# Stick-breaking attention: one log/softplus buffer per head parity, gate chunks split a step sooner, and TensorE's filler work in another order

## What is computed

```
z = einsum('bhqd,bhkd->bhqk', q, k) * scale
log_1m = where(strict, log_sigmoid(-z), 0)
tail = cumsum(log_1m, axis=3, reverse=True) - log_1m
a = where(strict, exp(log_sigmoid(z) + tail), 0)
sb = einsum('bhqk,bhkd->bhqd', a, v)
merged = sig(g_sb)*(sb @ w_up_sb) + sig(g_pl)*(pl @ w_up_pool) + sig(g_xa)*(xa @ w_up_x)
x += merged @ w_out ;  x += HierMoE(RMSNorm(x)) ;  out = RMSNorm(x)
```

## Time and profile before

| | before |
|---|---|
| median of 3 runs | 760.4 us (759.59 to 760.98) |
| profiled execution, its own time | 760.23 us |
| its span, first to last instruction | 758.5 us |
| mean granted TensorE clock | 0.972 |
| PE busy | 699.3 us (92%), 3547 matmuls |
| DVE busy | 514.1 us (68%) |
| ACT busy | 413.8 us (55%) |

### The profile page before, as it was taken

How to read it: one execution, slowest core, us unless ns; L and a number is a source line. 1 busy time by engine, 2 the same in 40 slices (tenths; PEclk the granted TensorE clock), 3 DMA queues, 4 the chain that set the end, 5 groups by cost and what they waited for, 6 DMA issues and landing times.

```text
span 758.5 us, 9936 instructions
## 1 busy us (share of the span) xinstructions
PE 699.3 (92%) x3547; PEld 583.3 (77%) x3547; DVE 514.1 (68%) x563; ACT 413.8 (55%) x428; POOL 109.6 (14%) x112
## 2 busy tenths in 40 slices
PE   4999999979799999999999989999999999999920
PEld 3898888878688888888888948888888888888810
DVE  5878755665534326071544588999999999999927
ACT  6726675675442323131233337777777778777712
POOL 5000000000000000000000130333433443331120
PEclk9999999998899999999999999999999999999975
DMA  8552330000042232233476369999999999999444
GB/s 282 170 167 56 111 111 1 1 28 2 15 149 87 83 111 79 87 97 125 165 264 236 122 217 393 394 388 370 367 375 369 366 376 366 385 366 375 181 170 189
DMA packets 85169, 155.47 MB, mean 205 GB/s; under 512 B 6229, under 2 KB 37071, under 8 KB 84628
## 3 DMA queue, kind: packets, MB, share of 16 engines
q1 hardware_dynamic: 78452, 137.39, 51.2%
q0 software_dynamic: 6688, 17.69, 6.2%
HBM read 150.64 MB, written 12.58 MB: 215 GB/s over the span
## 4 chain that ended last, share of the span: by engine, by line
PE 83%; DVE 6%; ACT 5%; issue 3%; DMA 2%; POOL 1%; POOLq 0%; DVEq 0%; ACTq 0%
PE ps L481 24%; PE ps L482 24%; PE ps L483 24%; PE ps L1536 2%; PE ps L1276 1%; PE ps L1278 1%; DVE soft L1826 1%; PE ps L1593 1%; PE ps L1462 1%; PE ps L1562 1%; PE ps L1490 1%; DMA y_rows<-ye,y_col 1%; ACT log_in L911 1%; ACT log_in L909 1%; ACT soft_hi L917 1%
## 5 line engine op out<-in xcount | busy, mean ns | idle before, releaser
L454 DVE TENSOR_TENSOR ring_lo<-raw_a,ring_hi 128x2048 fp32r<-128x2048 f32 (+2 forms) x58 | 115.5, 1995 | 103.6 <-ACT ring_hi L448 103.6
L454 DVE TENSOR_TENSOR ring_lo<-raw,ring_hi 128x2048 fp32r<-128x2048 f32 x71 | 161.4, 2289 | 12.3 <-ACT ring_hi L448 11.0
L448 ACT ACTIVATE ring_hi<-raw 128x2048 fp32r<-128x2048 f32 x71 | 136.2, 1920 | 19.8 <-PE ps L483 19.8
L481 PE MATMUL ps<-hT_hi,ring_hi 128*128 128x512 f32 x288 | 114.3, 397 | 5.3 <-ACT attn L923 3.4
L448 ACT ACTIVATE ring_hi<-raw_a 128x2048 fp32r<-128x2048 f32 (+2 forms) x58 | 97.4, 1680 | 32.3 <-PE ps L483 32.3
L483 PE MATMUL ps<-hT_hi,ring_lo 128*128 128x512 f32 x288 | 113.1, 393 | 0.0
L482 PE MATMUL ps<-hT_lo,ring_hi 128*128 128x512 f32 x288 | 113.1, 393 | 0.0
L481 PE MATMUL ps<-ring_hi,xT_hi 128*128 128x512 f32 x240 | 94.8, 395 | 1.8 <-DVE xT_lo L2039 1.8
L483 PE MATMUL ps<-ring_hi,xT_lo 128*128 128x512 f32 x240 | 93.8, 391 | 0.0
L482 PE MATMUL ps<-ring_lo,xT_hi 128*128 128x512 f32 x240 | 93.7, 390 | 0.0
L481 PEld LDWEIGHTS ps<-hT_hi,ring_hi 128*128 128x128 f32 x288 | 54.6, 190 | 17.8 <-ACT attn L923 3.6
(11 more groups left out here) (347 smaller groups left out, 1230.4 us busy)
## 6 DMA issues: line engine op xcount, KB each, us to landing
raw<-in_w_down SPq DMA_DIRECT2D x25, 1024.0 KB
raw<-in_w_gate SPq DMA_DIRECT2D x47, 512.0 KB
raw<-in_w_up SPq DMA_DIRECT2D x47, 512.0 KB
raw_a<-in_w_in SPq DMA_DIRECT2D x15, 1024.0 KB
raw_a<-in_w_gate SPq DMA_DIRECT2D x17, 512.0 KB
raw_a<-in_w_up SPq DMA_DIRECT2D x17, 512.0 KB
raw_a<-in_w_down SPq DMA_DIRECT2D x7, 1024.0 KB
raw_a<-in_w_in SPq DMA_DIRECT2D x10, 512.0 KB, 7.5
```

What stands on the lines that cost most here:

```text
L448: act.activation(ring_hi[:, c[0] % SPLIT, 0:width], buf[:, 0:width], ACT.Copy).then_inc(hi_ready, 1)
L454: dve.tensor_tensor(ring_lo[:, s, 0:width], buf[:, 0:width], ring_hi[:, s, 0:width].bitcast(F32), ALU.subtract).then_inc(lo_ready, 1)
L481: pe.matmul(out_ap, l_hi, r_hi, start=start, stop=False, skip_group_check=True)
```

## The change

Five things are edited. (1) `log_in` goes; the three passes of `logarithm(n)` and the softplus work in `soft[n % 2]`, with `soft_lo[n % 2]` on it, so that the two heads of a pair have a buffer each. `softplus` no longer waits for `tails(n-1)`; `soften` does instead, for `soft_hi`, which still exists once. (2) On DVE the softplus of an odd head is issued at the end of the pair before, not at the start of its own, and on ACT `soften(b)` stands ahead of `weigh(a)`. (3) The splits of chunks 10 and 11 move from the end of pairs 1 and 2 to their middle, ahead of `weigh(b)`, and `value_hi` and `value_lo` behind the logarithm and the softplus. (4) `fill_b` is cut in two at k = 2: 6 of its 24 matmuls (`CUT`) stand ahead of `values(b)`, 18 behind it; in pair 0 `project_v(2)` and `project_qk(5)` change places. (5) The gate half of the last pair goes to bank 7, the values of heads 6 and 7 to banks 2 and 3 (`value_bank`); the gate half waits for `value_sum(5)`, 15 of its 24 matmuls stand ahead of `tails(7)` and 9 behind `values(6)`. The number of matmuls is the same; ACT and DVE have one instruction less in each round of the gated sum, a pair of 512 columns becoming one of 1024.

```diff
@@ -210,9 +210,8 @@
     pool_a = sb("pool_a", [P, 2, U0 + S], F32, "t", 16 * KB + 8448)
     probs = [sb("probs0", [P, 8, MEM], F32, "m", 32 * KB), sb("probs1", [P, 8, MEM], F32, "t", 16 * KB)]
 
-    log_in = sb("log_in", [P, ZW], F32, "t", 0)
-    soft = sb("soft", [P, ZW], F32, "t", 5 * KB)
-    soft_lo = sb("soft_lo", [P, ZW], F32R, "t", 5 * KB)
+    soft = [sb(f"soft{b}", [P, ZW], F32, "t", 5 * b * KB) for b in range(2)]
+    soft_lo = [sb(f"soft_lo{b}", [P, ZW], F32R, "t", 5 * b * KB) for b in range(2)]
     soft_hi = sb("soft_hi", [P, ZW], F32R, "t", 10 * KB)
     attn_hi = sb("attn_hi", [P, ZW], F32R, "t", 15 * KB)
     attn = [sb(f"attn{b}", [P, ZW], F32, "t", (20 + 5 * b) * KB) for b in range(2)]
@@ -268,7 +267,10 @@
     def bank(b, n=1):
         return ps[:, 512 * b:512 * (b + n)]
 
-    GATE_BANK = ((6, 2), (0, 1), (4, 5))
+    GATE_BANK = ((6, 7), (0, 1), (4, 5))
+
+    def value_bank(m):
+        return bank(7 if m < HEADS - 2 else m - 4)
 
     def gate_pair(g):
 
@@ -904,17 +906,18 @@
             def logarithm(n):
 
                 act.wait_ge(z_ps, n + 1)
-                if n > 0:
-                    act.wait_ge(z_soft, n)
-                act.activation(log_in[:, :], scores(n), ACT.Abs).then_inc(act_c, 1)
+                buf = soft[n % 2]
+                act.activation(buf[:, :], scores(n), ACT.Abs).then_inc(act_c, 1)
                 act.wait_ge(act_c, 2 * n + 1)
-                act.activation(log_in[:, :], log_in[:, :], ACT.Exp, scale=-1.0).then_inc(act_c, 1)
+                act.activation(buf[:, :], buf[:, :], ACT.Exp, scale=-1.0).then_inc(act_c, 1)
                 act.wait_ge(act_c, 2 * n + 2)
-                act.activation(log_in[:, :], log_in[:, :], ACT.Ln, bias=1.0).then_inc(z_ln, 1)
+                act.activation(buf[:, :], buf[:, :], ACT.Ln, bias=1.0).then_inc(z_ln, 1)
 
             def soften(n):
                 act.wait_ge(z_soft, n + 1)
-                act.activation(soft_hi[:, :], soft[:, :], ACT.Copy).then_inc(soft_h, 1)
+                if n > 0:
+                    act.wait_ge(tail_ps, n)
+                act.activation(soft_hi[:, :], soft[n % 2][:, :], ACT.Copy).then_inc(soft_h, 1)
 
             def weigh(n):
                 act.wait_ge(tail_ps, n + 1)
@@ -937,14 +940,16 @@
             qk_hi(4, 6)
             for p in range(HEADS // 2):
                 a, b = 2 * p, 2 * p + 1
+                soften(b)
                 weigh(a)
-                soften(b)
                 if p == 0:
-                    qk_hi(5, 6)
+                    v_hi_part(2, 6)
                 if p == 1:
                     qk_hi(6, 6)
+                    split_hi(act, K(C_MERGE))
                 if p == 2:
                     v_hi_part(3, 6)
+                    split_hi(act, K(C_MERGE + 1))
                 weigh(b)
                 value_x(a)
                 if p < HEADS // 2 - 1:
@@ -952,18 +957,14 @@
                 value_x(b)
                 if p < HEADS // 2 - 1:
                     soften(a + 2)
-                value_hi(a)
-                value_hi(b)
                 if p == 0:
-                    v_hi_part(2, 6)
+                    qk_hi(5, 6)
                 if p == 1:
                     qk_hi(7, 6)
                 if p < HEADS // 2 - 1:
                     logarithm(b + 2)
-                if p == 1:
-                    split_hi(act, K(C_MERGE))
-                if p == 2:
-                    split_hi(act, K(C_MERGE + 1))
+                value_hi(a)
+                value_hi(b)
 
 
             act.preload_act_table_set("sigmoid_and_others")
@@ -1202,10 +1199,12 @@
                                         start=False, stop=m == MB - 1, skip_group_check=True)
                 ins.then_inc(xo_ps, 1)
 
-            def project_qk(n, b):
+            def project_qk(n, b, k0=0, k1=KD):
 
                 wh, wl = chunk(K(C_PAIR[n // 2]))
-                proj(b, wh, wl, 1024 * (n % 2), P).then_inc(chunk_used if n % 2 else q_ps, 1)
...
@@ -1283,7 +1282,7 @@
 
                 pr = m // 2
                 pe.wait_ge(a_l, m + 1)
-                if m >= 1:
+                if 1 <= m < HEADS - 2:
                     pe.wait_ge(av_sum, m)
                 if m == 0:
                     pe.wait_ge(v_l, 2)
...
@@ -1335,39 +1334,32 @@
 
             pe.wait_ge(xo_sum, 2)
             project_qk(4, 6)
-            def gate_part(k0, k1):
-
-                wh, wl = chunk(K(C_MERGE))
-                for k in range(k0, k1):
-                    o = P + k * 256
-                    ins = three(pe, bank(GATE_BANK[0][1]), wh[:, o:o + P], wl[:, o:o + P], hT_hi[:, k, :], hT_lo[:, k, :],
-                                k == 0, k == KD - 1)
-                return ins
+            CUT = 2
 
             def fill_a(p):
                 if p == 0:
                     pe.wait_ge(qk_l, 5)
-                    project_qk(5, 6)
+                    project_v(2, 6)
                 if p == 1:
-                    pe.wait_ge(v_l, 3)
+                    pe.wait_ge(qk_l, 6)
                     project_qk(6, 6)
                 if p == 2:
                     pe.wait_ge(qk_l, 8)
                     project_v(3, 6)
                 if p == 3:
-                    pe.wait_ge(a_exp, HEADS - 1)
-                    gate_part(0, KD // 2)
-
-            def fill_b(p):
+                    pe.wait_ge(av_sum, HEADS - 2)
+                    gate_half(0, 1, 0, None, 0, 5)
+
+            def fill_b(p, k0, k1):
                 if p == 0:
-                    pe.wait_ge(qk_l, 6)
-                    project_v(2, 6)
+                    pe.wait_ge(v_l, 3)
+                    project_qk(5, 6, k0, k1)
                 if p == 1:
                     pe.wait_ge(qk_l, 7)
-                    project_qk(7, 6)
+                    project_qk(7, 6, k0, k1)
                 if p == 2:
                     pe.wait_ge(v_l, 4)
-                    gate_half(0, 0, 0, None)
+                    gate_half(0, 0, 0, None, k0, k1)
 
             for p in range(HEADS // 2):
                 tails(2 * p)
@@ -1376,10 +1368,12 @@
                 values(2 * p)
                 if p < HEADS // 2 - 1:
                     scores_pair(p + 1)
+                    fill_b(p, 0, CUT)
                 else:
-                    gate_part(KD // 2, KD).then_inc(chunk_used, 1)
+                    gate_half(0, 1, 0, None, 5, KD).then_inc(chunk_used, 1)
                 values(2 * p + 1)
-                fill_b(p)
+                if p < HEADS // 2 - 1:
+                    fill_b(p, CUT, KD)
 
 
             def rest(d, dp):
@@ -1821,14 +1815,13 @@
 
             def softplus(n):
                 dve.wait_ge(z_ln, n + 1)
-                if n >= 1:
-                    dve.wait_ge(tail_ps, n)
-                dve.scalar_tensor_tensor(soft[:, :], bank(3 * (n % 2), 3)[:, 0:ZW], 0.0, log_in[:, :],
+                dve.scalar_tensor_tensor(soft[n % 2][:, :], bank(3 * (n % 2), 3)[:, 0:ZW], 0.0, soft[n % 2][:, :],
                                          ALU.max, ALU.add).then_inc(z_soft, 1)
 
             def soft_low(n):
                 dve.wait_ge(soft_h, n + 1)
-                dve.tensor_tensor(soft_lo[:, :], soft[:, :], soft_hi[:, :].bitcast(F32), ALU.subtract).then_inc(soft_l, 1)
+                dve.tensor_tensor(soft_lo[n % 2][:, :], soft[n % 2][:, :], soft_hi[:, :].bitcast(F32),
+                                  ALU.subtract).then_inc(soft_l, 1)
...
@@ -1853,20 +1846,22 @@
             split_lo(dve, K(C_V[1]))
             cross_o(1)
             qk_lo(4, 6)
+            softplus(1)
             for p in range(HEADS // 2):
                 a, b = 2 * p, 2 * p + 1
-                softplus(b)
+                soft_low(b)
                 weight_hi(a)
-                soft_low(b)
                 weight_lo(a)
                 if p == 0:
-                    qk_lo(5, 6)
+                    v_lo_part(2, 6)
                 if p == 1:
                     qk_lo(6, 6)
+                    split_lo(dve, K(C_MERGE))
                 if p == 2:
                     v_lo_part(3, 6)
+                    split_lo(dve, K(C_MERGE + 1))
+                weight_hi(b)
                 value_sum(a)
-                weight_hi(b)
                 weight_lo(b)
                 if p == HEADS // 2 - 1:
                     dve.sem_inc(b_used, 3)
@@ -1875,16 +1870,14 @@
                 value_sum(b)
                 if p < HEADS // 2 - 1:
                     soft_low(a + 2)
+                if p == 0:
+                    qk_lo(5, 6)
+                if p == 1:
+                    qk_lo(7, 6)
+                if p < HEADS // 2 - 1:
+                    softplus(b + 2)
                 value_lo(a)
                 value_lo(b)
-                if p == 0:
-                    v_lo_part(2, 6)
-                if p == 1:
-                    qk_lo(7, 6)
-                if p == 1:
-                    split_lo(dve, K(C_MERGE))
-                if p == 2:
-                    split_lo(dve, K(C_MERGE + 1))
 
 
             with dve.Fori(0, KD // 2) as dp:
```

(11 more changed lines are left out.)

23 lines of the change are left out of this document (8 added, 15 removed).

## The result

The changed kernel takes 749.21 us (median of 4 executions, 747.55 to 749.50) against 760.69 (4 executions, 759.59 to 761.23): ratio 0.9844, 95% interval 0.9826 to 0.9861, so 11.5 us faster. 747.8 was forecast, 745.5 to 755 as the range.

A forecast was written before the change was run, and what follows sets the result against it. PE was taken as the bound, busy behind the attention and idle only within it. values(7) moves from 208.45 to 195.9, a gain of 12.6 us: 760.2 - 12.6 = 747.6, or 747.8 on the median's scale; range 745.5 to 755.

The forecast's parts named there:

- a PE block of 15.3 or 15.6 us and a chain of 8.3: Attention: PE work from tails(a) to the scores' end, then the three-engine chain; 23.59 or 23.87 us a pair.
- The long stops and their falls: PE idle 3.58 us before tails(5) and 3.44 before the gate half, each with a clock fall; removal wins 6.3 and 6.0.
- Splits in mid-pair: Splits of chunks 10 and 11, 1.90 and 2.29 us, move without cost; cover before values(3) 0.6 us.
- Two buffers and the early softplus: Attention: the wait before tails(b) goes with 0.8 us to spare, removing the 3.58 us stop and its clock fall.
- The fill's cut: 6 matmuls cover the stop before values(b); nothing gained in time, a single 1.3 us stop before tails(a) remains.
- First rival: Clock falls at the new 1.3 us stops before tails(a): 750.5 to 755.8 us; chance 0.15, shared with late splits.
- matrix work behind the attention: Gates, branch products and experts, PE always busy: starts and ends earlier by all that the attention gives up, 12.6 us.

The follow-up runs named there:

- the lengthened chain: Changed kernel with one more ACT pass over 1280 columns (1.28 us) ahead of soften(2), soften(4) and soften(6): 755.08 us, ratio 0.9927 to the kernel before.
- the undivided filler: Changed kernel with all 24 matmuls of fill_b behind values(b), instead of 6 ahead and 18 behind: 748.38 us, ratio 0.9855 to the kernel before.

## Why the prediction was right, and where not

- *The pair is a PE block of 15.3 or 15.6 us and a chain of 8.3.* Right: the starts of `tails(a)` came within 0.1 us, the chain from the last scores to `tails(a)` measured 8.28 to 8.30 us, and the lengthened chain and the undivided filler confirm that the chain follows the PE block and nothing hides it.
- *The long stops and their falls.* Right in sum, 12.6 forecast, 12.5 measured at `values(7)`. The cause given for the second was half of it: "the gate half wants bank 2, which `weigh(6)` must leave". With bank 2 alone out of the way the kernel is slower by 1 to 3 us. `soft_low(7)`, late by the split of chunk 11, released `tails(7)` at the same moment, and the sum held only because the change removes both.
- *Splits in mid-pair, priced at nothing.* Right where they are now: the operand of `values(3)` was ready at 150.44 and PE came at 151.26, a cover of 0.8 us where 0.6 was forecast. Left at the end of the pairs they cost 5.4 us at `values(7)` in the profiled execution and 3.8 between the lowest ones, so this edit carries a third to a half of the gain.
- *Two buffers and the early softplus, credited with the stop of 3.58 us.* Not tested by themselves. With the splits left late, all other parts together shorten that stop to 1.14 us; whether the moved splits would have removed it without the second buffer stays open.
- *The fill's cut, priced at nothing.* Right: 195.86 against 195.92.
- *First rival, a fall at the 1.3 us stops.* Not seen: at 1.00 through all stops of 1.32 or 1.33 us before `tails(a)` in the profiled executions of the changed kernel and of all variants that have them. The Trainium skill's rule on frequent short idle times (TensorE: Matmul & The Clock Gate, "A second HAM failure mode: psum-queue depth-cycling") did not show at this length; stops of 1.53 to 2.63 us did bring the clock down, in some executions.
- *The step that was off* is the first: matrix work behind the attention "ends earlier by as much". It does in the executions without a fall (747.73 profiled, against 760.23 of before, is 12.5). By time and mean clock most of them have a fall or more, 1.5 us or more each, and the median gained 11.5. The kernel before has such executions too (its 27 executions of two series run from 759.13 to 764.04). Whether the changed kernel has more of them was not shown; its median stands 1.8 above its lowest (749.3 to 747.55), that of before 1.3 (760.4 to 759.13). Lowest against lowest the gain is 11.6 as well, because some executions of before have a higher mean clock (0.974 to 0.976) than its profiled one (0.972). So that the median fell 1.1 short of the 12.6 is not fully explained. The forecast of 747.8 is 1.4 below the median of 749.21.

## What to carry to other kernels

A stop has as many causes as there are chains that end near it. Before crediting one, date the next wait behind it: the released engine may only wait elsewhere, in one long stop, and the low clock may then lie on work that has no time to spare.

In a pipeline of several engines, name the chain that sets the pace and count what stands in it by order alone. A conversion that fits anywhere should stand where its engines have slack; filler belongs in the stop of the chain, not where PE already has time to spare.

Where executions of one kernel spread by steps, compare the lowest as well as the medians, and look at the granted clock of the profiled one before explaining a difference of one or two us. A profiled execution can be the slowest of its kernel, as in seven of the twelve runs here that are not the kernel before.
